# A hybrid decoder step with 32 experts: expert blocks of 96 rows, a short slot list, and numbering spread over the experts

## The reference

```python
n = rmsnorm(x, norm_attn)
q, k, v, gb, gc, hc = split(n @ w_in)          # 4 heads, two score maps each
s = q @ k.T * scale + t5_bias                  # causal, two maps
a = softmax(s[0]) - lam * softmax(s[1])
o = rmsnorm(a @ v, attn_subln) * (1 - lam_init)
c = rmsnorm(gb * causal_conv(gc * hc, conv_w), conv_norm)
h = x + concat(o, c) @ w_out
# hierarchical mixture of experts on xt = rmsnorm(h, norm_ffn)
g_sel = argmax(xt @ router_group)              # 1 of 4 groups
top_p, top_i = top_k(softmax(le[g_sel]), 2)    # 2 of its 8 experts
y = sum over the 2 experts e: comb[e] * ((silu(xt @ w_gate[e]) * (xt @ w_up[e])) @ w_down[e])
y_out = rmsnorm(h + y, norm_final)
```

## Time and profile before

| | |
|---|---|
| median of 3 runs | 1073.07 us |
| the profiled execution | 1070.95 us, span 1069.1 us |
| TensorE, matmuls | 916.2 us busy (86%) |
| VectorE | 577.2 us (54%) |
| ScalarE | 499.4 us (47%) |
| GpSimd | 442.3 us (41%) |
| HBM read and written | 171.19 and 42.34 MB |

### The profile page before, as it was taken

The page is one execution under the profiler, slowest core; times in us unless marked ns, Lnnn a source line. Parts: engine busy times, 40 slices in busy tenths (PEclk is TensorE's granted clock), DMA queues, the critical chain, the costliest instruction groups (busy, mean ns, idle before and its releaser), DMA issues.

```text
span 1069.1 us, 14098 instructions
## 1 busy us (share of the span) xinstructions
PE 916.2 (86%) x4937; PEld 749.7 (70%) x4937; DVE 577.2 (54%) x1032; ACT 499.4 (47%) x830; POOL 442.3 (41%) x332
## 2 busy tenths in 40 slices
PE   4899999999999999958969997289999999999700
PEld 3799887888788778845757665178888887777500
DVE  4504532353325332767645137787777767767347
ACT  4423344334433434253312121558888877777412
POOL 1102322222332323223313120078999975565475
PEclk9999999999999999979979998589999999999955
DMA  8033223232121103270253521989999999998785
GB/s 263 18 93 101 80 80 94 88 99 80 41 62 30 51 28 103 86 236 1 83 168 119 177 84 64 360 311 376 410 412 406 413 405 399 402 397 329 280 283 204
DMA packets 92554, 206.25 MB, mean 193 GB/s; under 512 B 12767, under 2 KB 54303, under 8 KB 84294
## 3 DMA queue, kind: packets, MB, share of 16 engines
q1 hardware_dynamic: 79950, 168.13, 43.3%
q10 hardware_dynamic: 5528, 20.04, 4.8%
q0 software_dynamic: 7008, 17.18, 4.5%
HBM read 171.19 MB, written 42.34 MB: 200 GB/s over the span
## 4 chain that ended last, share of the span: by engine, by line
PE 66%; DVE 10%; DMA 9%; issue 5%; POOL 4%; ACT 4%; SPq 2%; ACTq 0%; POOLq 0%; DVEq 0%
PE pj L971 25%; PE pj L1854 11%; PE pj L1060 7%; DMA e_raw<-in_w_up 7%; PE pj L1900 6%; PE pj L1037 5%; PE pj L1022 3%; POOL f_y L2112 2%; PE tp L1829 2%; PE tp L1011 1%; DVE e_lo L1806 1%; DVE sc L1253 1%; DMA k_page<-in_cache_k 1%; PE pj L1452 1%; PE tp L994 1%
## 5 line engine op out<-in xcount | busy, mean ns | idle before, releaser
L971 PE MATMUL pj<-n_hi,w_hi 128*128 128x350 f32 (+1 forms) x576 | 200.3, 348 | 3.4 <-DVE n_lo L1291 3.4
L1806 POOL TENSOR_TENSOR e_lo<-e_raw,e_hid 128x2048 fp32r<-128x2048 f32 x32 | 167.6, 5237 | 72.8 <-ACT e_hid L1802 72.7
L971 PE MATMUL pj<-n_lo,w_hi 128*128 128x350 f32 (+1 forms) x576 | 188.4, 327 | 0.0
L971 PE MATMUL pj<-n_hi,w_lo 128*128 128x350 f32 (+1 forms) x576 | 187.5, 325 | 0.0
L1806 DVE TENSOR_TENSOR e_lo<-e_raw,e_hig 128x2048 fp32r<-128x2048 f32 x64 | 148.6, 2324 | 0.1
L669 POOL TENSOR_TENSOR w_lo<-w_raw,w_hi 128x1024 fp32r<-128x1024 f32 x21 | 50.1, 2388 | 204.5 <-ACT w_hi L744 204.5
L1802 ACT ACTIVATE e_hig<-e_raw 128x2048 fp32r<-128x2048 f32 x64 | 122.7, 1919 | 25.3 <-DMA e_raw<-in_w_up 18.7
L971 PEld LDWEIGHTS pj<-n_hi,w_hi 128*128 128x128 f32 x576 | 109.7, 190 | 32.3 <-issue 30.4
L1253 DVE CUSTOM_DVE_ANT_0 sc<-pj,strip 128x512 f32<-128x512 f32 (+5 forms) x120 | 61.6, 545 | 102.1 <-PE pj L1037 60.6
L971 PEld LDWEIGHTS pj<-n_lo,w_hi 128*128 128x128 f32 x576 | 110.0, 191 | 0.6
L971 PEld LDWEIGHTS pj<-n_hi,w_lo 128*128 128x128 f32 x576 | 109.8, 191 | 0.7 <-issue 0.6
(11 more groups left out here) (257 smaller groups left out, 1710.8 us busy)
## 6 DMA issues: line engine op xcount, KB each, us to landing
e_raw<-in_w_up SPq DMA_DIRECT2D x32, 1024.0 KB, 18.3
e_raw<-in_w_gate SPq DMA_DIRECT2D x32, 1024.0 KB, 20.4
e_raw<-in_w_down SPq DMA_DIRECT2D x32, 1024.0 KB, 21.9
expert_rows<-yo ACTq DMA_DIRECT2D x32, 512.0 KB, 8.2
w_raw<-in_w_in SPq DMA_DIRECT2D x24, 512.0 KB, 3.9
expert_rows<-logits SPq DMA_DIRECT2D x16, 512.0 KB, 5.1
wo_raw<-in_w_out SPq DMA_DIRECT2D x8, 512.0 KB, 5.0
k_page<-in_cache_k SPq DMA_DIRECT2D x16, 256.0 KB, 3.8
```

Of the source, the lines that this page charges most:

```text
L971: ins = pe.matmul(pj[g % 2][:, 0:tn], ws[w][:, P * k:P * (k + 1)], x[:, k, t0:t0 + tn], start=(m == 0), stop=(m == 23))
L1806: eng.tensor_tensor(e_lo[r][:, q, :], e_raw[r][:, q, :], e_hi(par, q).bitcast(F32), ALU.subtract).then_inc(s_lo[q], 1)
```

## The change

- **Blocks of 96 rows** (`CB`). Gather, transposes, splits, products and stores have 96 rows for 128; a further block begins at the 97th token of an expert. The list has 22 further blocks for 16 (`XB`), so the final loop has 22 steps, and 22 zero fills of 96 rows for 16 of 128 in the attention part.
- **Short slot list.** `block_tok` has a column for each expert alone (32), made by `tokens` right after the choice. The rank serves as the place without a division into blocks, since a rank of 96 or more matches no column of `place_hot`. The 14 placement matmuls of the first seven tiles go before the last tiles' ranks. `s_slots` is raised after these 32 columns.
- **Numbering of further blocks** (`route_more`, 13 pieces): pieces 0 and 1 stand before VectorE's first split, pieces 2 to 12 in the loop, one in each odd expert from 5 to 25, between the product `hh` and VectorE's half of the copy. Its numbers lie in the bank `pj[2]`. TensorE's 18 matmuls for it (`pe_more`) stand behind experts 15, 19 and 23. The gates' arithmetic goes to the start of the final phase.
- **Choice of experts** with 4 instructions for 5 in each maximum (a descending code takes the place of an index), 2 for 3 in the mask.
- **Loads.** Experts 0 and 1 are asked for in slot 51, after the store of tile 7, in rotated buffers; expert 2 without a wait for the last logits; expert 3 after two gathers and no longer after the whole list. ScalarE rounds expert 0's weights in slot 54. ScalarE no longer fills `xg`.
- **First experts.** VectorE splits expert 1's weights before the first product; GpSimd's first split waits for that.
- **Score pairs.** Both matmuls of a piece wait for VectorE's last read of the piece before, and 12 fills stand between two pieces for 6.

```diff
-MAXB = 48
-XB = MAXB - NE
+CB = 96
+OV = -(-TOK // CB) - 1
+XB = 22
+MAXB = NE + XB
+assert XB >= 2 * TOK // (CB + 1)
 BIG = 1.0e30
+CODE = 95.0
...
+                if s == S_BACK + 1:
+                    sp.wait_ge(s_be, USE[("z", 0, 0)] + 1)
+                    for q in (1, 0, 2):
+                        load_piece(sp, 0, q, 0, 0, 0)
+                    sp.wait_ge(s_dm, MIXN[(NT - 1, 0)] + 1)
+                    for q in (1, 0, 2):
+                        load_piece(sp, 1, q, 1, 0, 1)
...
+                if s == S_BACK + 4:
+                    act.wait_ge(s_csl, 2 * NT)
+                    for q in (1, 0, 2):
+                        high(act, 0, q, 0, 0)
...
+            u = PIE[s] + 2 * p
+            if u >= 2:
+                pe.wait_ge(s_sb, u)
             for c in range(2):
-                u = PIE[s] + 2 * p + c
-                if u >= 2:
-                    pe.wait_ge(s_sb, u - 1)
...
-                        fill(ga, 6)
+                        fill(ga, 12)
...
+                    if i == NT - 1:
+                        route_rank(dve, did, 0, TE)
...
+                    if i == NT - 1:
+                        route_place(dve, did, 0, TE)
...
-                if s == S_EARLY + 1:
...
+        e_at = [r0 + 83456, r0, r0 + 24576, r0 + 49152]
...
+        rk = pj[2][:, 0:NR].rearrange("p (i c t) -> p i c t", i=7, c=2)
+        cnt = pj[2][:, NR:NR + NE]
+        nx_ps = pj[2][:, NR + NE:NR + 3 * NE]
+        nxs = at("nxs", [P, 2, 2 * NE], F32, o_junk)
+        hot_x = pj[2][:, NR + 3 * NE:NR + 3 * NE + NT * XB].rearrange("p (t x) -> p t x", x=XB)
...
-                do(dve.scalar_tensor_tensor(tmp, tmp, -64.0, over_rows(iota32, T, n), ALU.mult, ALU.add))
-                do(dve.tensor_reduce(idx, tmp, AX.X, ALU.min))
-                do(dve.tensor_scalar(idx, idx, 64.0, None, ALU.add))
+                do(dve.tensor_tensor(tmp, tmp, over_rows(code, T, n), ALU.mult))
+                do(dve.tensor_reduce(v, tmp, AX.X, ALU.max))
...
+            T = t1 - t0
+            dve.wait_ge(s_step, did.n[0])
+            for c in range(2):
+                did(dve.tensor_tensor(block_tok[:, c, t0:t1], hot2[:, c, t0:t1], each(C("token1")[:, t0:t1], T, NE), ALU.mult))
...
+            dve.wait_ge(s_step, did.n[0])
             for c in range(2):
-                did(dve.tensor_tensor(over2[:, c, t0:t1], each(rk[:, 0, c, t0:t1], T, 8), over_rows(C("over"), T, 8), ALU.is_ge))
-            dve.wait_ge(s_step, did.n[0])
-            do(dve.tensor_reduce(rk[:, 2, :, t0:t1], over2[:, :, t0:t1], AX.X, ALU.add))
-            do(dve.scalar_tensor_tensor(rk[:, 3, :, t0:t1], rk[:, 2, :, t0:t1], -float(P), rk[:, 0, :, t0:t1], ALU.mult, ALU.add))
-            for c in range(2):
-                dve.tensor_tensor(place_hot[:, c, t0:t1], over_rows(C("iota128"), T, P), each(rk[:, 3, c, t0:t1], T, P), ALU.is_equal).then_inc(s_ph, 1)
+                dve.tensor_tensor(place_hot[:, c, t0:t1], over_rows(C("iota128"), T, CB), each(rk0[:, c, t0:t1], T, CB), ALU.is_equal).then_inc(s_ph, 1)
...
+            route_rank(dve, did, TE, NT)
...
+            do(dve.tensor_copy(cnt, rank_ps[:, NT, :]))
+            dve.wait_ge(s_pm, 1)
+            do(dve.tensor_scalar(slot_f[0:CB, :], pj[1][0:CB, 0:NE], 0.0, 4096.0, ALU.is_equal, ALU.mult))
+            do(dve.scalar_tensor_tensor(slot_f[0:CB, :], pj[1][0:CB, 0:NE], -1.0, slot_f[0:CB, :], ALU.add, ALU.add))
+            do(dve.tensor_copy(slot_tok[0:CB, 0:NE], slot_f[0:CB, :]))
+            dve.sem_inc(s_slots, 1)
+
+        def route_more(dve, did, n):
...
-            do(dve.tensor_tensor(over_e, spread(rank_ps[:, NT, :], [[1, NE], [0, 8]]), over_rows(ov, NE, 8), ALU.is_gt))
-            do(dve.tensor_reduce(nx[0], over_e, AX.X, ALU.add))
-            for i, d in enumerate((1, 2, 4, 8, 16)):
-                do(dve.tensor_tensor(nx[(i + 1) % 2], nx[i % 2], nxs[:, i % 2, NE - d:2 * NE - d], ALU.add))
...
-            for c in range(2):
-                do(dve.tensor_tensor(block_hot[:, c], over_rows(C("iota128")[:, 0:MAXB], NT, MAXB), each(rk[:, 6, c], NT, MAXB), ALU.is_equal))
-                dve.tensor_tensor(block_tok[:, c], block_hot[:, c], each(C("token1"), NT, MAXB), ALU.mult).then_inc(s_ph, 1)
...
+            if n == 0:
+                did(dve.memset(nxs[:, :, 0:NE], 0.0))
+                did(dve.tensor_copy(rk[:, 0], rk0[:]))
+                do(dve.tensor_tensor(over_e[:], spread(cnt, [[1, NE], [0, OV]]), over_rows(C("over"), NE, OV), ALU.is_gt))
+                do(dve.tensor_reduce(nx[0], over_e[:], AX.X, ALU.add))
+            elif n == 1:
+                for i, d in enumerate((1, 2, 4, 8, 16)):
+                    do(dve.tensor_tensor(nx[(i + 1) % 2], nx[i % 2], nxs[:, i % 2, NE - d:2 * NE - d], ALU.add))
+                did(dve.tensor_copy(nx_ps, nxs[:, 1, :]))
+            elif n in (2, 3):
+                c = n - 2
+                do(dve.tensor_tensor(big_x[:], hot2[:, c], over_rows(below, NT, NE), ALU.mult))
+                do(dve.tensor_reduce(rk[:, 1, c], big_x[:], AX.X, ALU.add))
...
+            elif n == 5:
+                do(dve.scalar_tensor_tensor(flat[4], flat[2], 1.0, sb[1], ALU.min, ALU.mult))
+                do(dve.scalar_tensor_tensor(flat[5], flat[4], CODE, evf, ALU.add, ALU.subtract))
+                for c in range(2):
+                    do(dve.tensor_tensor(hot_x, over_rows(C("iota128")[:, NE:MAXB], NT, XB), each(rk[:, 5, c], NT, XB), ALU.is_equal))
+                    do(dve.tensor_tensor(tok_x[:, c], hot_x, each(C("token1"), NT, XB), ALU.mult))
+            elif n in (7, 9, 11):
+                if n > 7:
+                    dve.wait_ge(s_pm, n - 6)
+                for j in (n - 7, n - 6):
+                    c, t0 = j // 3, 3 * (j % 3)
+                    if j >= 2:
+                        dve.wait_ge(s_pm, j)
+                    dve.tensor_tensor(place_x[:, j % 2], over_rows(C("iota128"), 3, CB), each(rk[:, 3, c, t0:t0 + 3], 3, CB), ALU.is_equal).then_inc(s_ph, 1)
+            elif n == 6:
+                do(dve.tensor_copy(sb[2], flat[5]))
+                do(dve.scalar_tensor_tensor(flat[6], flat[3], float(MAXB), sb[2], ALU.mult, ALU.add))
+                did(dve.tensor_copy(addr[:], flat[6]))
...
+            elif n == 12:
+                dve.wait_ge(s_pm, 7)
+                do(dve.tensor_scalar(slot_x[0:CB, :], list_x, 0.0, 4096.0, ALU.is_equal, ALU.mult))
+                do(dve.scalar_tensor_tensor(slot_x[0:CB, :], list_x, -1.0, slot_x[0:CB, :], ALU.add, ALU.add))
+                did(dve.tensor_copy(slot_tok[0:CB, NE:MAXB], slot_x[0:CB, :]))
+                dve.wait_ge(s_step, did.n[0])
+                dve.sem_inc(s_slots, 1)
...
+        def act_gates(act):
+            act.wait_ge(s_rx, 6)
+            act.activation(grp[:, 2], grp[:, 1], ACT.Exp).then_inc(s_re, 1)
+            act.activation(gs[:, 4, :], gs[:, 2, :], ACT.Exp).then_inc(s_re, 1)
...
+            pe.wait_ge(s_t, 2 * NT)
+            for c in range(2):
+                pe.wait_ge(s_ph, c + 1)
+                for t in range(TE):
+                    pe.matmul(pj[1][0:CB, 0:NE], place_hot[:, c, t, :], block_tok[:, c, t, :], start=(c + t == 0), stop=False)
             pe.wait_ge(s_mark, 3)
-            pe.wait_ge(s_ph, 2)
...
-                pe.wait_ge(s_ph, 4 + c + 1)
-                for t in range(NT):
-                    ins = pe.matmul(pj[1][:, 0:MAXB], place_hot[:, c, t, :], block_tok[:, c, t, :], start=(c + t == 0), stop=(c + t == NT))
+                pe.wait_ge(s_ph, 2 + c + 1)
+                for t in range(TE, NT):
+                    ins = pe.matmul(pj[1][0:CB, 0:NE], place_hot[:, c, t, :], block_tok[:, c, t, :], start=False, stop=(c == 1 and t == NT - 1))
...
+        def pe_more(pe, n):
+            for j in (n - 7, n - 6):
+                c, t0 = j // 3, 3 * (j % 3)
+                pe.wait_ge(s_ph, 4 + n - 5)
+                for t in range(3):
+                    ins = pe.matmul(list_x, place_x[:, j % 2, t, :], tok_x[:, c, t0 + t, :], start=(j + t == 0), stop=(j + t == 7))
+                ins.then_inc(s_pm, 1)
...
-            act.dma_start(y_rows[:, bass.ds(n, 1), :], yo[:, par:par + 1, :]).then_inc(s_yst[par], 16)
+            act.dma_start(y_rows[:, bass.ds(n, 1), :], yo[0:CB, par:par + 1, :]).then_inc(s_yst[par], 16)
...
-            for n in range(2):
-                for q in (1, 0, 2):
-                    load_piece(sp, n, q, n, 0, n)
+            for q in (1, 0, 2):
+                load_piece(sp, 2, q, 2, 0, 2)
             sp.wait_ge(s_lge, NT)
             sp.wait_ge(s_hsq, NT)
-            for q in (1, 0, 2):
-                load_piece(sp, 2, q, 2, 0, 2)
-            sp.wait_ge(s_slots, 2)
-            for n in range(2):
-                sp.wait_ge(s_xg[n], 16)
+            for r in range(2):
+                sp.wait_ge(s_xg[r], 16)
...
+                if n == 0:
+                    pool.wait_ge(s_lo[0], 2)
...
+                    route_more(dve, did, 0)
+                    route_more(dve, did, 1)
```

(9 more changed lines are left out.)

263 lines of the change are left out of this document (133 added, 130 removed).

## The result

| | before | changed |
|---|---|---|
| median | 1073.07 us | 1062.7 us (1057.27 to 1063.41) |
| profiled execution | 1070.95 us | 1057.27 us, span 1055.4 |

The ratio is 0.989 (95% interval 0.9862 to 0.9919). The kernel is faster by 10 us; I had forecast 29, and the range (1033 to 1058) missed the time.

The account below looks back on a forecast made before the run. Attention was taken as TensorE-bound, routing as a chain of short VectorE instructions, the expert loop as narrowly DMA-bound. Savings of 6.8 + 13.2 + 9.4 = 29.4 us from 1070.95 gave 1041.6, or 1043.7 us as median; range 1033 to 1058.

Parts of the forecast that it names:

- The loop, -9.4: Expert loop: smaller 96-row stores save 9.4 us of DMA time over 29 stores; bounds -3 and -14.
- a TensorE cycle of 9.1 us: Expert loop: eight transposes of 96 columns take 0.2 us less, so TensorE's cycle of 9.33 us becomes 9.1.
- Rival 3: Expert loop: numbering pieces do not fit VectorE's waits and push the copy and TensorE; +14 us, 1058 us; chance 0.07.
- Rival 1: Expert loop: the store's saved bytes do not become time (half the ports, or weight reads limit); 1052.1 us; chance 0.12.
- Rival 2: Attention: score pairs bring nothing, as the later second piece moves the softmax; 1050.5 us; chance 0.09.
- Routing, -13.2: Last tile's norm to slot list: earlier ranks, shorter choice, no numbering before the list; saves 13.2 us, bounds -15 and -10.
- The 0.6 ahead of the mark: Routing: shorter choice of experts on the earlier five tiles saves 0.6 us, part of the 13.2.
- The gather's 4.6 and the 4.7 from first transpose to first expert matmul stay: Slot list to first expert matmul: both times unchanged, with VectorE's splits of expert 0 no later.
- Score pairs, -6.8: Attention: paired waits and 12 fills save 7.8 us in three heads, net 6.8; bounds -11 and 0.
- Numbering: Expert loop: eleven pieces of 1 to 2 us hide in VectorE's waits, three 1 us matmul groups beside late loads.
- The end, 0: Final phase: six more loop steps, at most 4.1 us, stay hidden under GpSimd's 10.99 us wait for the last store.
- Rival 4: Final overflow loop runs for an expert with over 96 tokens, about 36 us each; 1080 us for one; chance 0.02.

Follow-up runs that it names:

- s64_low: Changed kernel without storing rows 64 to 95 of each expert's store (zero-filled in the attention part instead): 1065.11 us, ratio 0.9928.
- s64_mid: Changed kernel without storing rows 0 to 31 of each expert's store (zero-filled in the attention part instead): 1063.75 us, ratio 0.993.
- n128_s96: Changed kernel without numbering pieces 7 to 12, half of 5, their matmuls and the final loop; blocks and gathers of 128 rows, stores of 96: 1051.75 us.
- g128: Changed kernel with gathers of 128 slots for 96, the added slots reading no row; stores stay at 96 rows: 1051.98 us, ratio 0.982.
- g112_skip: g128_skip with gathers of 112 slots for 128: 1061.74 us, ratio 0.9903.
- g128_skip: g128 with the final loop inside a test, so no step runs without a further block: 1051.2 us, ratio 0.9807.
- old_pairs: Changed kernel with score pairs as before: each matmul waits for its own bank, 6 fills between pieces; 1064.09 us, ratio 0.9937.
- load2_late: Changed kernel with expert 2's loads asked for after the first gather has landed, ahead of expert 3's: 1061.79 us, ratio 0.9906.
- best_low: g128_skip with 7 fills in slots transposing next head's keys or values, VectorE's expert 1 split in its old place, GpSimd's first split not waiting: 1045.17 us.
- num6: Changed kernel without numbering pieces 7 to 12, half of piece 5, the three groups of numbering matmuls and the final loop: 1060.19 us, ratio 0.9887.
- psum_pieces: g128_skip with the operands of numbering pieces 10 and 12 in PSUM: 1052.84 us, ratio 0.9816.

## Why the prediction was wrong

- **The loop, -9.4.** This is the step that failed: +2.9 and +6.0. "The 96-row store has 0.393 MB for 0.524 ... 9.4 us" has the right mechanism and too high a price: 32 rows of a store are worth 3.1 us (s64_low, s64_mid) and 3.4 (n128_s96) of late loads, where all late loads of before were 7.1. And I priced the bytes of blocks of 96 and not the gather's shape. It reads the same rows, so it stood in no term, and it costs 4.5 and 7.6 us of loop (g128 against the two traces of the changed kernel) and 8.9 (g112_skip against g128_skip), besides some 2 at the first gather. The second half of the term, a TensorE cycle of 9.1 us, is wrong as well: it is 9.36, for transposes of 96 columns take the 0.80 us of 128, and the products for down 2.78 for 2.73. My lower bound of -3 excluded a loss, and that closed the range.
- **The loop without that gather.** Even then the term fails: g128's loop is 309.0 us, 1.6 less than before. Its excess is 5.2 lower (7.1 to 1.9, what is left being the numbering). But its first two cycles take 2.4 more, and 1.3 more of cycle 0 lies behind the first product, since the stretch from first transpose to first product is 3.4 for 4.7.
- **The rivals.** Rival 3's 1058 us is nearest to the time, by luck: its cause, pieces that stall TensorE, is worth 0.4 us. Rival 1 had the loop failing, as it did, for a reason that the runs speak against: a store's bytes do turn into time, wherever they lie. Rival 2 did not occur (old_pairs).
- **Routing, -13.2.** Of it 12.6 lay behind the mark, and 12.2 came; the stretch from the last logits took 7.96 us for the 8 forecast. The 0.6 ahead of the mark did not show: old_pairs reaches it no earlier than before.
- **"The gather's 4.6 and the 4.7 from first transpose to first expert matmul stay".** The sentence began so, and the list came early enough for the gather to meet the loads: 8.1 us for 4.6 (load2_late, g128). The 4.7 became 3.4. That expert 0's products took 1.5 us more in the first trace and 0.1 in the second stays unexplained.
- **The first experts** had no term at all. VectorE's split of expert 1 ahead of the first product costs 3.6 us in the first two cycles and 1.1 in the loop (best_low).
- **Score pairs, -6.8.** -3.3. The pieces gained nearly what I said, 2.3 us a head for 2.6 (0.4 for each longer piece, 0.6 for the 1.0 of tile 4), but three heads gave -4.4 for -7.8. I did not ask where six more fills per piece are taken from. For the last head I had net +1.0 (tile 4 -1.0, the rest +2.0), and it was +1.1 between the start of tile 4 of that head and the residual.
- **Numbering.** "Beside loads that are late anyway" fits the groups of matmuls: on the path by 0.51 us each, and worth nothing when left out (num6). Rival 3 was right on 2 of 11 pieces, and they cost 0.4 us where no load is late, which did not come back as a gain (psum_pieces).
- **The end, 0.** I took a step's length from GpSimd's wait and covered six more with it; VectorE has its own loop, and the landed gather is its limit. It costs nothing or some 4 us, by the chip.
- **Rival 4** did not occur: 32 loads of each kind.

## What to carry over

When a loop is bound by the DMA, look at each transfer's shape as well as its bytes, and test the new shape alone: a gather is 0.268 of an expert's 3.807 MB, and its shape slowed the whole DMA by 4%. Work taken off an engine behind a full DMA returns as waiting, so first find what is late last. When filler is moved to cover one wait, list whose cover it was.

## What the hardware showed that I had not expected

- An indirect gather of 96 or 112 slots for 128, with the same rows read, cut the whole DMA rate from 397 to 399 GB/s to 381 to 386, at the same busy share of 1.01 to 1.02. With no loads in front such a gather is as fast as before (4.55 us, load2_late).
- Empty steps of a loop on VectorE took 0.54 us each in most traces and 0.75 in four, all of one chip.
- A VectorE instruction of 22 columns within SBUF took 4.13 us beside GpSimd's product, while a reduction within SBUF beside one took 0.52.
